# One program for the output stage and the experts of a hybrid decoder layer on Trainium2

## What is computed

```python
y = concat(gla_o, nsa_o) @ w_out
x = x + mod[2] * y
h = rmsnorm(x, g_ffn) * (1 + mod[4]) + mod[3]
logits = h @ w_router + b_router
top_logit, top_idx = top_k(logits, 4)          # 4 of 32 experts
top_w = softmax(top_logit)
# every expert, for the rows that chose it, in blocks of up to 128 rows:
gate = min(h_e @ w_gate[e] + b_gate[e], 7)
up   = clip(h_e @ w_up[e] + b_up[e], -7, 7)
f   += top_w * (((up + 1) * gate * sigmoid(1.702 * gate)) @ w_down[e] + b_down[e])
y = rmsnorm(x + mod[5] * f, g_final)
```

## Time and profile before

| | us |
|---|---|
| median of 3 runs | 1803.28 (1802.6 to 1803.57) |
| profiled execution | 1810.53 |
| its span | 1808.5 |
| granted clock, mean | 0.96 |

### The profile page before, as it was taken

The page is one execution under the profiler, slowest core; times in us unless marked ns, Lnnn a source line. Parts: engine busy times, 40 slices in busy tenths (PEclk is TensorE's granted clock), DMA queues, the critical chain, the costliest instruction groups (busy, mean ns, idle before and its releaser), DMA issues.

```text
span 1808.5 us, 27028 instructions
## 1 busy us (share of the span) xinstructions
PE 1692.2 (94%) x9028; PEld 1315.4 (73%) x9028; DVE 1424.4 (79%) x1356; ACT 1103.4 (61%) x1052; POOL 331.5 (18%) x309
## 2 busy tenths in 40 slices
PE   4999978888998779999999999999999999999996
PEld 2776757655554568888888888888888888888884
DVE  4422564477425879999999999999999999999996
ACT  4212343354334366777777777777777777777773
POOL 0000021300101012122212312222231222223211
PEclk9999999699998679999999999999999999999998
DMA  9454553520226479999999999999999999999993
GB/s 350 166 184 174 101 157 97 194 110 2 76 91 186 171 278 327 381 376 375 368 381 375 373 374 376 378 371 373 382 373 374 388 371 370 389 369 375 384 348 124
DMA packets 114598, 516.08 MB, mean 285 GB/s; under 512 B 25870, under 2 KB 47710, under 8 KB 62058
## 3 DMA queue, kind: packets, MB, share of 16 engines
q1 hardware_dynamic: 101082, 483.48, 70.8%
q0 software_dynamic: 12800, 29.45, 5.9%
q10 hardware_dynamic: 656, 2.36, 0.3%
HBM read 502.75 MB, written 31.09 MB: 295 GB/s over the span
## 4 chain that ended last, share of the span: by engine, by line
PE 61%; DVE 1%; DMA 1%; ACT 0%; issue 0%; SPq 0%; POOL 0%; DVEq 0%; POOLq 0%; ACTq 0%
PE banks L2965 57%; PE banks L2973 3%; PE banks L2951 1%; DMA routing<-in_g_final 0%; DMA ffn_rows<-weighed,block_rows 0%; DVE split L3167 0%; DVE arena L3264 0%; PE banks L3020 0%; ACT split L3079 0%; DVE arena L3257 0%; DVE arena L3256 0%; SPq L2885 0%; POOL wait_taken L2903 0%; DVEq L2831 0%; DVE gates L3180 0%
## 5 line engine op out<-in xcount | busy, mean ns | idle before, releaser
L2965 PE MATMUL banks<-split 128*128 128x512 f32 x4608 | 1076.7, 393 | 1.1 <-DVE split L3167 1.1
L2965 PEld LDWEIGHTS banks<-split 128*128 128x128 f32 x4608 | 860.7, 188 | 186.2 <-issue 7.2
L3167 DVE TENSOR_TENSOR split<-expert_buffers,split 128x2048 fp32r<-128x2048 f32 x384 | 864.7, 2283 | 42.5 <-ACT split L3079 40.2
L3079 ACT ACTIVATE split<-expert_buffers 128x2048 fp32r<-128x2048 f32 x384 | 733.3, 1918 | 217.0 <-PE banks L2965 212.8
L2903 POOL TENSOR_TENSOR wait_taken<-routing 128x1 f32<-128x1 f32 x62 | 76.3, 1230 | 812.0 <-PE banks L2973 464.5
L2926 POOL DMA_INDIRECT ffn_rows<-weighed,block_rows x31 | 107.7, 3473 | 4.8 <-issue 4.6
L662 PE MATMUL banks<-w_in_high,hT_high 128*128 128x476 f32 x192 | 76.0, 396 | 4.2 <-DVE hT_low L498 4.2
L3171 DVE TENSOR_TENSOR split<-banks,split 128x1024 fp32r<-128x1024 f32 x64 | 77.7, 1214 | 0.7 <-ACT split L3082 0.7
L662 PE MATMUL banks<-w_in_high,hT_low 128*128 128x476 f32 x192 | 73.4, 382 | 0.0
L3082 ACT ACTIVATE split<-banks 128x1024 fp32r<-128x1024 f32 x64 | 64.5, 1008 | 6.0 <-PE banks L2973 6.0
L573 DVE COPY arena<-banks 128x476 f32<-128x476 f32 x12 | 7.8, 653 | 70.0 <-PE banks L662 70.0
(11 more groups left out here) (396 smaller groups left out, 1739.8 us busy)
## 6 DMA issues: line engine op xcount, KB each, us to landing
expert_buffers<-in_w_gate SPq DMA_DIRECT2D x128, 1024.0 KB, 8.1
expert_buffers<-in_w_up SPq DMA_DIRECT2D x128, 1024.0 KB, 5.0
expert_buffers<-in_w_down SPq DMA_DIRECT2D x128, 1024.0 KB, 7.7
arena<-in_w_ada SPq DMA_DIRECT2D x16, 1024.0 KB, 5.0
w_in_landing<-in_w_in SPq DMA_DIRECT2D x5, 1904.0 KB, 8.9
arena<-in_w_ada SPq DMA_DIRECT2D x4, 2048.0 KB, 20.0
arena<-in_x_prompt SPq DMA_DIRECT2D x8, 512.0 KB, 7.1
arena<-in_cache_cmp SPq DMA_DIRECT2D x32, 128.0 KB, 3.0
```

The lines of the kernel that those rows point to most:

```text
L2965: last = pe.matmul(ps[:, bank + c, :], x[:, kt * P:(kt + 1) * P].bitcast(F32R), wt.bitcast(F32R), start=(m == 2 and kt == 0 and x is xs[0] ...
L3079: act.activation(high[:, j % RING_Q].bitcast(F32R), v, ACT.Copy).then_inc(s_high, 1)
L3167: dve.tensor_tensor(rest[:, j % RING_Q].bitcast(F32R), v, high[:, j % RING_Q], ALU.subtract).then_inc(s_rest, 1)
```

## The change

The two stages become one program, `output_and_experts`. `output_and_router` turns into `router_programs`, which returns the five engines' parts, and each engine of the expert program calls its part first. There is no meeting of the engines and no clearing of semaphores between them.

- The rows of block 0 no longer come from HBM. `take_rank` writes 0/1 marks (`in_first`, token by place in expert 0's block), and `first_rows` multiplies each tile's normed rows by them on TensorE, which gives block 0's rows already turned. The order of TensorE is changed: `ranks` of tile t-2 stand between the halves of `project_out(t)`, `first_rows(t-2)` between `turn_rows` and `route`. For that all five tiles of normed rows have places of their own.
- The root comes from Sqrt and a reciprocal instead of Ln and Exp. VectorE multiplies by the scale row before it waits for the root. `choose`, `take_rank` and `place` of the last two tiles come after the last norm; `place` takes two tiles at once, has a third part for the weight's low bits, and its products are rounded ones (F32R).
- SP asks for the first three quarters after the last output product and for three more after the last norm, ahead of the store of the last rows.
- The shares' turning, the table and the initial sums stand between the quarters of block 0 (sums 3 and 4 in block 1). ScalarE's readings of the sums are put among its roundings.
- The block counts and the overflow's placing and table move to step `COUNT_AT` = 16. Up to there the loops have constant ends and block k is expert k; from 17 on they use the counted ends.

```diff
-    core.s_xg = core.sem("rows_gathered", carry=True)
+    core.s_xg = core.sem("rows_gathered")
...
+        def first_rows(t):
+
+            n = TILES[t][1]
+            pe.wait_ge(s_in_first, t + 1)
+            v = h2[t].rearrange("s (p k) -> s k p", k=KT)
+            for kt in range(KT):
+                last = pe.matmul(ps[:, 6 + kt // 4, (kt % 4) * P:(kt % 4 + 1) * P], v[0:n, kt, :], in_first[t][0:n, :],
+                                 start=(t == 0 and kt % 4 == 0), stop=(t == ST and kt % 4 == 3))
+                if t == ST and kt == KT // 2 - 1:
+                    last.then_inc(s_half, 1)
...
+        for t in range(NT):
+            project_out(t, range(KT // 2))
+            if t >= 2:
+                ranks(t - 2)
+            project_out(t, range(KT // 2, KT))
...
+            if t >= 1:
+                turn_rows(t - 1)
                 if t >= 2:
+                    first_rows(t - 2)
+                route(t - 1)
+        turn_rows(ST)
+        ranks(ST - 1)
+        route(ST)
+        ranks(ST)
+        first_rows(ST - 1)
+        first_rows(ST)
+        ranks(NT)
...
-            link(act.activation(dummy, core.const("one"), ACT.Ln))
+            link(act.activation(dummy, core.const("one"), ACT.Sqrt))
...
+            one = first1[0:m, t:t + 1]
+            link(dve.scalar_tensor_tensor(one, ps[0:m, 3, t * NE:t * NE + 1], 1.0, selb[0:m, t, 0:1], ALU.add, ALU.mult))
+            dve.tensor_scalar(in_first[t][0:m, :], core.const("iota_p")[0:m, :], 1.0, one, ALU.add, ALU.is_equal
+                              ).then_inc(s_in_first, 1)
...
+            def first_block():
+                pe.wait_ge(s_ones, 1)
+                pe.wait_ge(router.s_lg, NT)
+                pe.wait_ge(router.s_cnt, 1)
+                start_with_bias(0, 1, GB)
+                start_with_bias(1, 1, UB)
+                pe.wait_ge(s_xt, 1)
+                product(0, (xh, xl), GB, 0, range(2))
+                turn_shares(range(ST))
+                pe.wait_ge(s_xt, 2)
+                product(0, (xh, xl), GB, 0, range(2, 3))
+                turn_shares(range(ST, NT))
+                product(0, (xh, xl), GB, 0, range(3, 4))
+                product(1, (xh, xl), UB, 4, range(1))
+                tables()
+                product(1, (xh, xl), UB, 4, range(1, 2))
+                begin_sums(0)
+                product(1, (xh, xl), UB, 4, range(2, 3))
+                begin_sums(1)
+                product(1, (xh, xl), UB, 4, range(3, 4))
+                begin_sums(2)
+                turn_rows(1, first=True)
+
+            def step(k, prev, last=False, counted=False):
                 gate(k, first_of(prev))
+                if is_zero(prev):
+                    begin_sums(3)
                 turn_act(k)
+                if counted:
+                    pe.wait_ge(s_y, prev)
+                    overflow()
                 up(k, first_of(prev) + 4)
+                if is_zero(prev):
+                    begin_sums(4)
...
             sigmoid(0)
             high_part(7, None)
-            for j in range(2):
-                high_part(j, 0)
+            high_part(0, 0)
+            begin_read(0)
+            high_part(1, 0)
+            begin_read(1)
+            high_part(2, 0)
+            begin_read(2)
             rows_T(1)
-            for j in range(2, 4):
-                high_part(j, 0)
+            high_part(3, 0)
...
             rest_part(0, None)
+            take_rank(ST)
+            take_counts()
+            first_rest_T()
+            dve.wait_ge(router.s_bo, 16)
+            rest_part(1, None)
+            last_shares()
+            rest_part(2, None)
+            last_places()
+            rest_part(3, None)
+            shares_low()
+            for j in range(4, 7):
                 rest_part(j, None)
...
+                if count:
+                    count_blocks(core, dve, linker(dve, s_dve, dve_count)).then_inc(s_counted, 1)
+                    place_overflow(core, dve, linker(dve, s_dve, dve_count)).then_inc(s_over, 1)
                 for j in range(4, 7):
                     rest_part(j, prev)
...
             step(1, 0)
+            with dve.Fori(2, COUNT_AT) as k:
+                step(k, k - 1)
+            step(COUNT_AT, COUNT_AT - 1, count=True)
+            dve.wait_ge(s_counted, 1)
+            nb, nb1, nb2, _ = used_blocks(dve)
+            with dve.Fori(COUNT_AT + 1, nb1) as k:
                 step(k, k - 1)
```

More of the change, by code:

```diff
@@ L2241, in output_and_router @@
     gffn, br, junk = own.take(D), own.take(NE), own.take(D)
-    h2 = own.take(2 * D).rearrange("p (u n) -> p u n", u=2)
-    own = Stack(core, late.at, core.z1 - 2 * PAST // PAGE * 256)
-    ex_out = [core.arena[:, hole[0] + 512:hole[0] + 512 + D], own.take(D)]
-    ex_ffn = [core.arena[:, at:at + 2 * D].rearrange("p (v n) -> p v n", v=2) for at in hole[1:3]]
+    h2 = [own.take(D) for _ in range(2)] + [gffn]
+    z_turned = own.at - 416
+    small = Stack(core, core.z_moe + LANDING * QK * D + 368, core.z_moe + LANDING * QK * D + 512)
+    low4, wt4 = (small.take(2 * TOPK).rearrange("p (t j) -> p t j", j=TOPK) for _ in range(2))
+    vals = small.take(2 * TOPK * 3).rearrange("p (m w) -> p m w", w=3)
+    wsum, first1 = small.take(NT), small.take(NT)
+    own = Stack(core, ARENA - N_SPLIT, ARENA - N_SPLIT + 2 * QK * D)
+    h2 += [own.take(D), junk]
+    bdown = own.take(D)
     h2T = own.take(KT * P).rearrange("p (k n) -> p k n", k=KT)
@@ new lines, in router_programs @@
+    s_in_first, s_half, s_xtp = (core.sem(n) for n in ("first_block_marked", "first_half_ps", "xT_ps"))
+    s_bg, s_bga = core.sem("begin_ps"), core.sem("begin_read")
+    s_begun = [core.sem(f"begin_out{i}") for i in range(3)]
+    part = Programs()
+    part.s_yp, part.s_rk, part.s_tab, part.s_bga, part.s_begun, part.s_bo, part.s_xtp, part.s_half, part.s_gate2, part.s_h2o = (
+        s_yp, s_rk, s_tab, s_bga, s_begun, s_bo, s_xtp, s_half, s_gate2, s_h2o)
+    part.s_lg, part.s_cnt, part.s_bs, part.s_ew = s_lg, s_cnt, s_bs, s_ew
@@ L2714 @@
+    part.sync, part.gpsimd, part.tensor, part.scalar, part.vector = sync, gpsimd, tensor, scalar, vector
+    return part
 LIMIT, ALPHA = 7.0, 1.702
@@ L3072, in _ @@
         def _(act):
+            router_rows_T, weights, shares_T, begin_read = router.scalar(act)
             def high_part(j, prev):
@@ L3130, in step @@
                 sigmoid(k)
+                if is_zero(prev):
+                    begin_read(3)
+                    for i in range(2):
+                        act.wait_ge(s_begun[i], 16)
                 acts_T(k)
```

979 lines of the change are left out of this document (508 added, 471 removed).

## The result

| | before | after |
|---|---|---|
| median | 1803.42 (4 runs, 1802.6 to 1803.75) | 1814.91 (4 runs, 1810.92 to 1817.52) |
| ratio | | 1.0061 [1.0044, 1.0078] |
| span of the profiled execution | 1808.5 | 1809.3 |
| mean granted clock | 0.96 | 0.967 |

The change makes the kernel slower by 0.6%, 11 us. The forecast was 1803.7 with a range of 1793 to 1811: the time lies outside it, on the side of "slower", to which 0.25 was given. A repetition of both kernels beside the experiments gave 1.0046 [1.0028, 1.0065].

A forecast was written before the change was run, and what follows sets the result against it. TensorE was taken as the bound, gapless in the expert blocks at 35.09 us each. A gain of 9.7 us by block 2 and a loss of 10.1 in block 16 gave +0.4, so 1803.7 us, range 1793 to 1811.

The forecast's parts named there:

- slower: Outcome side covering rivals B and C together, against a forecast of no change; chance 0.25.
- Output stage and first product: Up to block 0: last rows at 609.9 instead of 614.5, first expert product at 623.5 instead of 646.92, 23.4 us earlier.
- The marks' products: TensorE, output stage: 16 records cost 1.86 us at full clock, 3.65 at half; the last 32 taken as 5.8.
- Blocks 0 and 1: After the first product: much is given back; gate of block 1 at 664.2, block 2 at 704.8, 9.7 us gained.
- The gather: GpSimd's gather of block 1's rows starts at the table, lands 3.5 us after issue, at 657.3 to 659, just hidden.
- Block 16: New place of counts and overflow: 8.5 us plus a clock fall of 1.6 as in block 0 before, 10.1 together.
- The table's mechanism: Block 16: VectorE's read up, table and activation come late; quarter 11 ready 1.7 late, the next first quarter 0.2.
- The sum: Whole kernel: -9.7 by block 2 and +10.1 in block 16 give +0.4 us, so 1803.7, no change.
- A: Rival, faster: holes cost no clock (1.6 + 1.6), block 1 ordering hidden (3.4), marks' products at full clock (2); chance 0.36.
- B: Rival, slower: half clock in gapped block 0, up to 7 us before block 1's gate; 1807 to 1813; chance 0.22.
- C: Rival: early start lost whole, block 2 starts as before, block 16's 10.1 paid in full, 1813; chance 0.03.
- the four counts: TensorE reading four numbers of blocks at the loop's end: bounds 0 and 4.2 us, taken as 0.

The follow-up runs named there:

- table_before_up: Changed kernel with VectorE writing the overflow's table in block 16 right after reading the gates, not the ups; ratio to before 1.0031 [1.0013, 1.0049].
- spread: Changed kernel with counting and overflow placing cut into nine pieces over blocks 8 to 16, table as in table_before_up; ratio to before 1.0014 [0.9997, 1.0032].
- round7_first: Changed kernel with ScalarE rounding quarter 7 of block 0 before the sigmoid; ratio to before 1.0061 [1.0040, 1.0083].
- counts_at_3: Changed kernel with counts, overflow placing, products and table in block 3 instead of block 16; ratio to before 1.0056 [1.0040, 1.0072].
- no_counts: Changed kernel without counts and the overflow's places, products and table, loops ending at constant 32; 1796.68 us, ratio to before 0.9969 [0.9951, 0.9987].
- no_overflow_products: Changed kernel without TensorE's 40 overflow products, the table's writing and waits; VectorE still counts and places in block 16; ratio to before 1.0016 [1.0000, 1.0031].
- mixed_in: spread with the 40 small products split behind quarters 4, 5 and 6 of block 16, table behind the activation's split; ratio to before 1.0006 [0.9992, 1.0020].
- reordered: mixed_in plus round7_first's edit and, in block 1, the fifth initial sum read before quarter 11's rounding; ratio to before 0.9986 [0.9972, 1.0001].
- table_between: reordered with the overflow's table written between quarters 9 and 10 of block 16 instead of ahead of quarter 8; ratio to before 0.9981 [0.9968, 0.9993].

## Why the prediction was wrong

**Output stage and first product: right.** 78.7 us into the stage was predicted for the first product, 79.8 measured. Two terms were mis-sized, and that they partly cancel is luck. The marks' products were priced like routing products, 16 in 1.97 at full clock; 16 of them took 3.97 (from 598.14), and the 32 from 610.19 took 8.34 where 5.8 was taken, right ahead of the first expert product. VectorE was earlier than its sum: the last rows were ready at 64.0 us into the stage and not at 65.1, and the last marks' products began 1.5 earlier than predicted. TensorE had no room in the middle of the stage either (42.81 of 43 us busy).

**Blocks 0 and 1: right within 2 us.** Most waits are those named: VectorE 2.93 before quarter 7 (3.0 predicted), TensorE 3.25 before the first sum (3.4 predicted), the gate's split rows 2.37, one fall of the clock (13.50 for 48 products, 2.3 above a steady block; 1.6 was taken). The gather was predicted to be just hidden, its rows landing 3.5 us after the issue. They land 5.96 after it, and TensorE waits 2.99. The gate of block 1 is 1.9 us late by this, since the fall of the clock, 1.6 in the sum ahead of the gate, comes behind it. Block 1 itself was predicted at 40.6 and took 40.5, with other terms: the wait behind ScalarE's last reading is 1.67 and not 3.4, that for the third quarter doesn't show, and the fall of the clock is in it. In sum 8.0 us won instead of 9.7, in this profile.

**Block 16: the step that failed.** Predicted 10.1, measured 14.05, and 14.1 in the repetition. The step is the fall of the clock, priced at the 1.6 us that follows the same products in block 0 of before. It costs 4.6 here: 1.8 in the 40 products, during which it begins, and 2.8 in the up product behind them. The other terms, with 0.2 of broken overlap for each wait: the wait for the places was right (1.95 predicted, 1.9 measured); the 40 products, priced at the 4.66 of the earlier trace rows, add 4.8 at full clock; the table costs 2.7 where 1.9 was taken. So 3.0 of the 3.95 us that were missing are the clock and 0.8 the table.

The 1.6 came from a block with other gaps and was carried to a filled one. What the same 40 products bring differs between profiles. Counted as what the granted clock falls short of full, by stretches of 5 us as above, it is 3.4 us in table_before_up and spread, 5.1 in after, 5.1 and then 1.7 more in round7_first, and 6.8 in counts_at_3. For the fall in block 0 of before the row gives 1.5 (4 us times 0.38), below all of them. Why it is more than in block 0, and why it differs, stays open.

The table's mechanism was wrong too. It was thought to make quarter 11 1.7 late; instead it holds up the down product itself by 2.47. The prediction counted VectorE's queue (read up, table, activation) and what comes after it; it did not ask who waits for the table. That is TensorE's down product: in the block that counts, `down` waits for the table (`s_tab`) ahead of its first quarter. It has to, since `overflow` puts its sums into bank `DB` of PSUM, which the down product fills next.

**The sum.** With 14.05 for 10.1 and 8.0 for 9.7, the prediction's own sum would have been +6.1 and not +0.4, so 1809.4, and "slower". The two terms explain 5.7 of the 11.2 us between forecast and median. The repetition, 8.3 us (5.1 to 11.7) above before, contains 6.1; the first comparison, 11.0 (7.9 to 14.1), does not, though it contains the 8.3 by which the second pair of profiles differs from the start of the stage to the end. What is left, some 2 to 5 us, is not settled. One part is seen: the output stage of the changed kernel runs in two ways. Seven of the eleven profiles of kernels that leave this stage as the change made it have block 0 at 78.2 to 79.2, three at 82.9 to 83.4, and one at 81.6. The granted clock tells them apart, 24 to 30 us into the stage, here in after and in no_counts:

```profile
564.00:570.00 6.00, 6.00 (x16) 2.59 (x15) 4.80 (x22) 0.13 (x1) 0.00 (x0) 0.95 0.89 212
...
565.00:571.00 6.00, 6.00 (x11) 2.42 (x10) 3.83 (x13) 1.34 (x2) 0.62 (x1) 0.64 0.77 270
```

At block 2 it is 3.4 us between the two ways, a mean of about 1 us over the eleven. TensorE has no gap behind it to hide slow products in: it is busy 38.00 of 38 us from 564 to 602 in no_counts. Before's two profiles both show a low clock there (0.64). That the rest is the length of the stages ahead of the change, which moves by 11.8 us between profiles, can't be shown with one profile per kernel.

**The rivals.** A fell on two of its three conditions: the holes do cost clock, and the marks' products are slow. Of the third, the 3.4 us in block 1, half came true (1.67). Its granted clock of 1.00 between 625 and 665 was 0.93. B fell too: that stretch isn't at 0.5, and from the first expert product to the gate of block 1 it is 41.5 us where 40.7 were predicted. The rule of the Trainium skill, page "TensorE: Matmul & The Clock Gate", part 1, that the throttled state is the default and activity releases it, agrees with the fall behind the holes of block 0 (13.50) and behind the 3.80 us of no_overflow_products. It doesn't by itself foresee the fall in spread, where TensorE had no gap. C was far off: block 2 starts 8 us earlier. The result has the sign of B and C, by a mechanism that none of the rivals held: the price of block 16 itself, which stood in the sum as a single number with no range of its own beside the 1.6 and the four counts. The four counts that TensorE reads cost nothing that shows, since block 17 begins without a bracket (the row at 1242.34).

## What to carry to other kernels

Work moved from a stage with idle time into a filled loop costs its full length and what it does to the others. Here waits and small products made 9.4 of the 14.05 us, and the fall of the clock the other 4.6. Put such work in pieces between full products, on VectorE as on TensorE, and write a result where no engine stands waiting for it: block 16 went from 49.1 to 39.9 us with the same 40 products and the table in it, and the blocks 8 to 15, which took over eight of the nine pieces of VectorE's work, stayed at 35.09. When a step is put into a queue, ask first who waits for its result, and only then what stands behind it.

## What the runs showed of the hardware

- TensorE's granted clock fell behind 40 small fp32 products (128x34) in one run, with no idle time before them: 5.00 us of them, then 0.60 and 0.72 granted, and 14.02 us for 48 products that take 11.2. In three groups of 8 or 16 with 12 split products between them it stayed at 1.00 (mixed_in, reordered, table_between).
- The weight loads of the marks' products (`first_rows`) took 336 ns each at either clock, and the products came 0.25 us apart, 16 in 3.97 us. Their stationary rows are read with a stride of eight words. Loads of the same size from rows that lie together took 190. But `turn_rows` (L2415) reads the same strided rows, for a transpose, in 192, so the stride alone isn't the cause; what is, stays open. From the groups of after, by line (engine and operation, ns min/median/max, first and last start, forms):

```profile
L2483 PEld LDWEIGHTS banks<-arena x80: 308/336/340, 570.6 to 617.9; 128*128 128x128 f32 x64, 64*128 64x128 f32 x16
...
L2415 PEld LDWEIGHTS banks<-arena x40: 183/192/207, 556.9 to 605.0; 128*128 128x128 f32 x32, 64*128 64x128 f32 x8
...
L2437 PEld LDWEIGHTS banks<-arena x64: 186/190/337, 540.2 to 582.4; 128*128 128x128 f32 x64
```

- The same stages of the same program ended between 535.3 and 547.1 us from profile to profile, and the repeated runs of before spread from 1797.4 to 1809.4. A difference of 0.2% needs gates counted from a common start, not two spans.
